# The samples' state scaled before its first use, and the decays' rows of all heads transposed once and broadcast from memory

## The chip, the cores and the metric

One kernel on one core of a Trainium2 chip. The metric is the device time of one execution in microseconds (us), lower is better. TensorE is called PE here, its weight loads PEld, VectorE DVE, ScalarE ACT, GpSimd POOL and SyncE, which issues most of the DMAs, SP.

## What is computed

One inference step of a hybrid decoder layer, for a prompt of 512 tokens and 8 samples of one token each. The width is 2048. One input projection feeds two mixers of 8 heads by 128: dilated window attention (A), and gated DeltaNet (B). The outputs go through a gate, one output projection and a norm. Everything is float32. The parts of mixer B that matter here are these two:

```python
# prompt: decay matrix of a chunk, from the cumulated logarithms of the per-head decays
gcum = jnp.cumsum(gc, axis=-1)
decay = jnp.exp(jnp.where(incl, gcum[..., :, None] - gcum[..., None, :], -jnp.inf))
a_mat = jnp.where(strict, einsum('bhnid,bhnjd->bhnij', kbeta, kc) * decay, 0.0)
...
# samples: one step on the state S (k x v) that each sample brings along
v_new = u_i - einsum('bhcd,bhde->bhce', w_i, state)
o_i = einsum('bhcd,bhde->bhce', q_i, state) + einsum('bhcj,bhje->bhce', qk_i, v_new)
state = state * gt_i[..., None, None] + einsum('bhcd,bhce->bhde', k_i, v_new)
```

`w_i` and `q_i` carry the token's decay `exp(g)`, so for one token all three terms with the state are terms with the decayed state: `v_new = beta (v - k S')`, the new state is `S' + k v_new`, and the output is `q` times the new state, where `S' = exp(g) S`.

## The kernel before

**Order of the work.** Two axes are walked: head by head (h = 0 to 7), and in each head 8 tiles of the input projection (j = 0 to 7). A tile is computed in 8 segments, 4 groups of the contraction for the first 256 tokens and 4 for the other 264. Every engine runs its own program through the same 64 turns of a head: in each turn `step(work)` advances a list of generators, each of which issues what stands up to its next `yield`. `yield from idle(n)` lets n turns pass. So the order on each engine is written out by hand, and engines meet by semaphores only. Heads 1 to 7 are a hardware loop on all engines but PE. In the text, "turn n" is the n-th of the 64 calls of a head, from 0; turn n of PE follows its segment n. A generator that begins with `idle(24)` issues its first work in turn 24.

**The projection.** Each weight tile is loaded (`w_raw`), ACT makes its high part (`w_hi`, function `hi`, L1029), and DVE and POOL take turns to make the low part (`w_lo`, function `lo`, L1396 and L2006). PE multiplies high and low parts with both parts of the tokens (L651 to L659). SP reloads `w_raw` once a low part is done (`wait_lo`). DVE takes the first half of a tile out of PSUM (L1427), ACT the second (L1059).

**The decay matrix.** `gates` (first head only) makes the cumulated logarithms of the decays of all heads, `G6[:, 1]` (128 tokens x 4 chunks x 8 heads). POOL copies those of the head into `hg`. In turn 23 PE transposes the keys (L802) and then the four columns `hg[:, 1, c]`, each spread over 128 columns (L806), which gives rows in PSUM, the same in every partition, in `mx(3)`. In turn 24 DVE subtracts the column from them (L1626) into `b_D` and masks (L1627); ACT takes the exponential (L1236). In turn 25 DVE makes `b_kb` from the keys (L1635), and PE transposes that in turn 26 (L816). `b_D` is last read in its head by DVE at L1726, turn 37, which signals `mix_QK`.

**The solve.** From turn 34 on, six levels n = 1 to 6 of a triangular inverse take three turns each: PE's product L844 (turn 34, 37, 40, 43, ...), ACT's copy, PE's L853, ACT's copy, DVE's update L1676 (turn 35, 38, 41, ...), PE's transposes L859 and DVE's update L1680 (turn 36, 39, 42, ...). The next L844 waits for both updates (`mix_UT`). POOL makes the masked operand of a level (L2055).

**The samples' state.** `delta_decode` on four engines. SP loads the keys' rows of the head, spread over the partitions (`k_rows`, L520, turn 19), the state `S0` (L526, turn 24), the queries' rows (`q_rows`, L534, turn 38), and stores the state (L538, turn 47). DVE reduces state times keys in turns 35 and 36 (L1740 in `fused`, eight blocks), makes small vectors of width 8 in turn 37 (L1777 to L1783), adds the update to the state in turns 41 to 43 (L1787, blocks 0 to 2, 3 and 4, 5 to 7), and reduces state times queries in turns 44 to 46. ACT scales the state by the decay in turns 37 and 38 (L1285, four blocks each) between the two. `fused` writes its products to `q_rows`, which are not used.

**SP's queue** around turns 16 to 24 of a head: four small stores of the keys, the probabilities' rows out (L444), a conv row out (L481), a weight load, the output of mixer A of the head before (`scratch_g<-gA`, L512, turn 18), the probabilities' rows in, three times 512 KB (L449, turns 19 to 21), and `k_rows`.

Of the kernel before, what the change touches and what calls it, by code (L numbers as in the profile page):

```python
# [157 lines left out]
def idle(n):  # L158
    for _ in range(n):
        yield  # L160
# [13 lines left out]
def build(nc, x_prompt, x_sample, cache_k, cache_v, state_conv, state_delta, g_pre, w_in, w_ba, conv_w, a_log, dt_bias,  # L174
# [5 lines left out]
    scratch_dq = nc.dram_tensor("scratch_dq", (NH, NB, HD), F32, kind="Internal").ap()  # L180
    scratch_g = nc.dram_tensor("scratch_g", (KT, P, TP), F32, kind="Internal").ap()

    with ExitStack() as ctx:
# [52 lines left out]

        small = sb("small", [P, 4 * P])
# [4 lines left out]
        gw = small[:, 0:160].rearrange("p (a c h) -> p a c h", a=4, c=NC + 1)  # L242
        gt = small[:, 160:240].rearrange("p (c a h) -> p c a h", a=2, c=NC + 1)
# [9 lines left out]
        k_rows = gx[:].rearrange("p a t -> p (a t)")  # L253
        q_rows = sb("q_rows", [P, WA])
# [73 lines left out]
        def mx(n):  # L328
# [17 lines left out]
            "hg_ok mix_T1 mix_ss mix_lnrk mix_rs mix_scal mix_gb mix_tok mix_kbT_ps mix_kbT mix_arg mix_D "  # L346
# [27 lines left out]
        def _(sp):  # L374
# [138 lines left out]

            def delta_decode(h):
                yield from idle(16)
                sp.wait_ge(s["q_row"], 3 * h + 1)
                rows_to(scratch_dk[h])
                yield from idle(3)
                sp.wait_ge(s["qrow_out"], 192 * h + 64)
                sp.dma_start(k_rows, scratch_dk[h].rearrange("b d -> (b d)").partition_broadcast(P)).then_inc(  # L520
                    s["dk_in"], 16)
                yield from idle(5)
                if not isinstance(h, int) or h > 0:
                    sp.wait_ge(s["S0_out"], 16 * h)
# [12 lines left out]
                sp.wait_ge(s["d_add"], h + 1)  # L537
                sp.dma_start(st_s[0, :, h].rearrange("b e d -> e b d"), S0[:]).then_inc(s["S0_out"], 16)  # L538
# [17 lines left out]
            stretch(0, [conv_out(0), attn_out(0), attn_rows(0), delta_decode(0)])  # L556
            with repeat(sp, 1, NH - 1) as h:
                stretch(h, [rows_out(h - 1), attn_decode(h - 1), conv_out(h), attn_out(h), attn_rows(h), delta_decode(h)])
            h = NH - 1
            stretch(h, [rows_out(h - 1), attn_decode(h - 1), conv_out(h), attn_out(h), attn_rows(h), delta_decode(h),  # L560
# [62 lines left out]
        def _(pe):  # L623
# [104 lines left out]
            def gates():  # L728

                yield from idle(8)  # L730
                pe.wait_ge(s["proj_sb"], 3)
                pe.wait_ge(s["consts"], 80)
                pe.wait_ge(s["memset_ok"], 2)
                for c in range(NC):
                    pe.matmul(MX[:, 0, c * 16:(c + 1) * 16], xba[:, c * P:(c + 1) * P], two_parts[:], start=True,
                              stop=True)
                pe.matmul(MX[0:NB, 0, 64:80], xba[:, TP:TT], two_parts[:], start=True, stop=True).then_inc(
                    s["gates_pe"], 1)
                yield from idle(5)
                pe.wait_ge(s["gates_dve"], 2)  # L740
                g = gw[:, 3, 0:NC, :].rearrange("p c h -> p (c h)")
                pe.matmul(MX[:, 1, 0:32], upper[:], g, start=True, stop=True)
                pe.matmul(MX[:, 1, 32:64], ones[:], g, start=True, stop=True).then_inc(s["gates_pe"], 1)
                yield from idle(3)
                pe.wait_ge(s["gates_dve"], 5)
                pe.matmul(MX[:, 0, 0:P], ones[0:NB, :], dgs.rearrange("p a h b -> p (a h b)"), start=True,
                          stop=True).then_inc(s["gates_pe"], 1)
# [43 lines left out]
            def mix_b(h):  # L791
# [12 lines left out]
                pe.wait_ge(s["hg_ok"], h + 1)  # L804
                for c in chunks:
                    last = pe.transpose(mx(3)[:, c, :], hg[:, 1, c:c + 1].to_broadcast((P, P)), ident[:])  # L806
                last.then_inc(s["mix_gb"], 1)
# [106 lines left out]
            def delta_decode(h):  # L914
# [6 lines left out]
                yield from idle(14)  # L921
# [96 lines left out]
        def _(act):  # L1018
# [116 lines left out]
            def gates():  # L1135
# [24 lines left out]
                act.wait_ge(s["gates_pe"], 3)  # L1160
                act.activation(bgs[:].rearrange("p a h b -> p (a h b)"), MX[:, 0, 0:P], ACT.Copy).then_inc(
# [116 lines left out]
            def delta_decode(h):  # L1278
                yield from idle(36)
                act.wait_ge(s["d_sum"], h + 1)  # L1280
                rsqrt(dd[:, 9:11, :], MD[:, 1, 0:2 * NB].rearrange("p (a b) -> p a b", a=2), 1.0, s["d_rs"])
                yield
                act.wait_ge(s["d_ks"], h + 1)
                for b in range(NB):
                    last = act.activation(S0[:, b, :], S0[:, b, :], ACT.Copy, scale=dd[:, 11, b:b + 1])  # L1285
                    if b == 3:
                        yield
                last.then_inc(s["S0_scaled"], 1)
                yield from idle(11)
                act.wait_ge(s["d_sq"], h + 1)  # L1290
                rsqrt(dd[:, 10, :], MD[:, 1, 16:24], 1.0 / HD, s["d_rs2"])
# [98 lines left out]
        def _(dve):  # L1390
# [230 lines left out]
            def mix_b(h):  # L1621
# [3 lines left out]
                dve.wait_ge(s["mix_gb"], h + 1)  # L1625
                link(dve.tensor_tensor(b_D, mx(3), bc(hg[:, 1, :]), ALU.subtract))  # L1626
# [123 lines left out]
            def delta_decode(h):  # L1750
# [4 lines left out]
                if not first:  # L1755
                    dve.wait_ge(s["qrow_out"], 192 * h)
                dve.transpose(qrow[:], xk[:, TT - 32:TT]).then_inc(s["q_row"], 1)
                yield from idle(18)
                dve.wait_ge(s["q_silu"], h + 1)
                if first:  # L1760
                    dve.wait_ge(s["gates_act"], 5)
# [4 lines left out]
                dve.tensor_copy(bt_s(0), bgs[:, 0, h, :])  # L1766
                dve.tensor_copy(bt_s(1), bgs[:, 1, h, :])
# [3 lines left out]
                dve.wait_ge(s["S0_in"], 16 * h + 16)  # L1771
# [6 lines left out]
                link(dve.tensor_tensor(dd[:, 6, :], dd[:, 6, :], bt_s(1), ALU.mult))  # L1778
# [5 lines left out]
                yield from idle(4)  # L1784
                dve.wait_ge(s["S0_scaled"], h + 1)
                for b in range(NB):
                    last = dve.scalar_tensor_tensor(S0[:, b, :], k_rows[:, b * P:(b + 1) * P], dd[:, 4, b:b + 1],  # L1787
                                                    S0[:, b, :], ALU.mult, ALU.add)
                    if b in (2, 4):
                        yield  # L1790
                last.then_inc(s["d_add"], 1)
                yield
                dve.wait_ge(s["d_add"], h + 1)
                dve.wait_ge(s["dq_in"], 16 * h + 16)
                yield from fused(None, q_rows, q_rows, dd[:, 1], (3, 6))
# [3 lines left out]
                yield from idle(3)  # L1799
# [77 lines left out]
            with repeat(dve, 1, NH) as h:  # L1877
                ch.at(h, 1, 49)
# [248 lines left out]
```

## Time and profile before

| | |
|---|---|
| Median of 3 runs | 1182.35 us (1182.23 to 1183.67) |
| The profiled execution | 1183.6 us |
| its span, first to last instruction | 1181.8 us |
| PE busy | 1146.7 us, 97% |
| DVE busy | 828.2 us, 70% |
| ACT busy | 492.8 us, 42% |
| POOL busy | 276.2 us, 23% |
| TensorE clock granted | 0.995 of full speed |
| DMA | 172.63 MB, 146 GB/s over the span |

The profile is one execution. "Busy" is the union of an engine's instructions; products on PE overlap, so starts of instructions tell more than their durations. A wait is put down to the event that came last before the waiting instruction. "DMA to landing" is the time from the issue on the queue to the semaphore that tells of the arrival.

### The profile page before, as it was taken

How to read it: one execution, taken by the hardware profiler on the slowest of the kernel's cores; microseconds unless marked ns; L12 is line 12 of the kernel's file. 1: busy time of each engine (PE TensorE's matmuls, PEld its weight loads, DVE VectorE, ACT ScalarE, POOL GpSimd, SP SyncE). 2: the span in 40 equal slices, each digit the busy share in tenths (PEclk: the TensorE clock that was granted, in tenths of full speed). 3: DMA queues.
4: the chain of work that ended last, by engine and by line, in shares of the span. 5: the costliest groups of instructions: out<-in, count | busy, mean ns of one | idle time of the engine just before them, and what ended most of it. 6: DMA issues, size and time to landing. Idle time of an engine off the chain costs nothing.

```text
span 1181.8 us, 24834 instructions
## 1 busy us (share of the span) xinstructions
PE 1146.7 (97%) x8241; PEld 1066.8 (90%) x8241; DVE 828.2 (70%) x2226; ACT 492.8 (42%) x1272; POOL 276.2 (23%) x251
## 2 busy tenths in 40 slices
PE   4999999999999999999999999999999999999997
PEld 4899989998999899989998999899998989999996
DVE  4587578777776777677777776778676877665544
ACT  5544345533543454344434443444344445322211
POOL 0223112311231123113211221222122212221211
PEclk9999999999999999999999999999999999999999
DMA  7243446344635363536253625453545374523263
GB/s 254 88 117 99 146 137 197 101 152 130 206 91 171 111 216 91 181 98 217 84 181 120 204 86 186 124 184 104 178 119 180 109 270 139 161 72 107 72 215 145
DMA packets 86635, 172.63 MB, mean 146 GB/s; under 512 B 14034, under 2 KB 24115, under 8 KB 84979
## 3 DMA queue, kind: packets, MB, share of 16 engines
q1 hardware_dynamic: 85246, 169.92, 45.5%
q10 hardware_dynamic: 1312, 1.59, 0.4%
q8 instruction: 60, 0.98, 0.4%
q14 instruction: 17, 0.13, 0.0%
HBM read 153.17 MB, written 17.44 MB: 144 GB/s over the span
## 4 chain that ended last, share of the span: by engine, by line
PE 88%; DVE 5%; issue 3%; ACT 2%; DMA 1%; SPq 0%; DVEq 0%; ACTq 0%
PE PJ L655 20%; PE PJ L651 11%; PE PJ L652 11%; PE PJ L653 11%; PE PJ L656 10%; PE MX L844 2%; PE PJ L956 2%; PE PJ L957 2%; PE MX L765 2%; PE PJ L958 2%; PE MX L853 2%; PE MX L785 1%; PE PJ L659 1%; DVE kvq L1824 1%; DVE S L1787 1%
## 5 line engine op out<-in xcount | busy, mean ns | idle before, releaser
L655 PE MATMUL PJ<-h,w_hi 128*128 128x512 f32 x1110 | 418.6, 413 | 1.4 <-DVE memx L1427 1.4
L2006 POOL TENSOR_TENSOR w_lo<-w_raw,w_hi 128x512 fp32r<-128x512 f32 x160 | 216.3, 1352 | 795.9 <-ACT w_hi L1029 795.1
L651 PE MATMUL PJ<-h,w_hi 128*128 128x264 f32 (+1 forms) x1216 | 359.7, 296 | 0.0
L652 PE MATMUL PJ<-h,w_hi 128*128 128x264 f32 (+1 forms) x1216 | 345.8, 284 | 0.0
L653 PE MATMUL PJ<-h,w_lo 128*128 128x264 f32 (+1 forms) x1216 | 345.4, 284 | 0.0
L656 PE MATMUL PJ<-h,w_lo 128*128 128x256 f32 x1110 | 311.0, 280 | 0.0
L655 PEld LDWEIGHTS PJ<-h,w_hi 128*128 128x128 f32 x1110 | 209.0, 188 | 44.2 <-DVE w_lo L1396 1.7
L1029 ACT ACTIVATE w_hi<-w_raw 128x512 fp32r<-128x512 f32 x320 | 196.8, 623 | 86.7 <-PE PJ L653 73.5
L652 PEld LDWEIGHTS PJ<-h,w_hi 128*128 128x128 f32 x1216 | 230.5, 190 | 1.5
L651 PEld LDWEIGHTS PJ<-h,w_hi 128*128 128x128 f32 x1216 | 230.2, 189 | 0.3
L653 PEld LDWEIGHTS PJ<-h,w_lo 128*128 128x128 f32 x1216 | 229.2, 188 | 0.0
L656 PEld LDWEIGHTS PJ<-h,w_lo 128*128 128x128 f32 x1110 | 209.4, 189 | 2.8 <-issue 1.7
L1396 DVE TENSOR_TENSOR w_lo<-w_raw,w_hi 128x512 fp32r<-128x512 f32 x160 | 117.0, 737 | 37.6 <-ACT w_hi L1029 34.9
L1598 DVE SCALAR_TENSOR_TENSOR memx<-memx,cw 128x512 f32<-128x512 f32 x72 | 74.9, 1041 | 2.0
L1045 ACT ACTIVATE memx<-memx 128x520 f32<-128x520 f32 x32 | 20.4, 637 | 117.1 <-DVE memx L1604 117.1
L1427 DVE TENSOR_REDUCE memx<-PJ 128x256 f32<-128x512 f32 x63 | 43.2, 686 | 28.8 <-DMA out<-memx 28.5
L1244 ACT ACTIVATE mem<-MX 128x256 f32<-128x256 f32 x48 | 18.4, 384 | 106.5 <-PE MX L844 106.5
L1824 DVE CUSTOM_DVE_ANT_0 kvq<-kvq 128x128 f32<-128x128 f32 x192 | 59.5, 365 | 0.3 <-DMA kvq<-in_cache_win_k 0.3
L2055 POOL TENSOR_TENSOR mem<-mem,levels 128x256 f32<-128x256 f32 x48 | 44.0, 922 | 31.4 <-PE MX L844 16.1
L956 PE MATMUL PJ<-h,w_hi 128*128 128x256 f32 (+1 forms) x160 | 47.6, 298 | 2.2 <-DVE h L1885 2.1
L1676 DVE TENSOR_TENSOR mem<-mem 128x256 f32<-128x256 f32 x40 | 23.4, 585 | 34.6 <-ACT mem L1248 34.1
L957 PE MATMUL PJ<-h,w_hi 128*128 128x256 f32 (+1 forms) x160 | 45.8, 286 | 0.0
(320 smaller groups left out, 1680.4 us busy)
## 6 DMA issues: line engine op xcount, KB each, us to landing
w_raw<-in_w_in SPq DMA_DIRECT2D x256, 256.0 KB, 2.8
w_raw<-in_w_out SPq DMA_DIRECT2D x64, 256.0 KB, 2.9
kvq<-in_cache_win_k SPq DMA_DIRECT2D x24, 512.0 KB, 4.7
kvq<-in_cache_win_v SPq DMA_DIRECT2D x24, 512.0 KB, 4.0
mem<-scratch_p SPq DMA_DIRECT2D x24, 512.0 KB, 7.0
out<-memx SPq DMA_DIRECT2D x16, 260.0 KB, 4.8
mem<-in_x_prompt SPq DMA_DIRECT2D x4, 1024.0 KB, 10.1
gx<-scratch_dk SPq DMA_DIRECT2D x8, 512.0 KB, 6.3
```

Of the source, the lines that this page charges most:

```text
L651: pe.matmul(ps, wh, h_hi[:, k, tok], start=k == 0, stop=False)
L652: pe.matmul(ps, wh, h_lo[:, k, tok], start=False, stop=False)
L653: last = pe.matmul(ps, wl, h_hi[:, k, tok], start=False, stop=end)
L655: pe.matmul(both, wh, h2[:, :, k, tok], start=k == 0, stop=False)
L656: last = pe.matmul(ps, wl, h_hi[:, k, tok], start=False, stop=False)
L956: pe.matmul(out, wh, h_hi[:, k, tok], start=start and i == 0, stop=False)
L957: pe.matmul(out, wh, h_lo[:, k, tok], start=False, stop=False)
L1029: act.activation(w_hi[:, par, 4 * q:4 * q + 4, :], w_raw[:, q, :, :], ACT.Copy).then_inc(s["w_hi_ok"], 1)
L1396: dve.tensor_tensor(w_lo[:, par, 4 * q:4 * q + 4, :], w_raw[:, q, :, :], w_hi[:, par, 4 * q:4 * q + 4, :].bitcast(F32), ALU.subtract).then ...
L1598: link(dve.scalar_tensor_tensor(acc[:, 0:TP], xq[:, i:i + TP], w[:, 24 + i:25 + i], acc[:, 0:TP], ALU.mult, ALU.add))
L1824: last = dve.tensor_tensor_reduce(out=x, in0=x, in1=qb[:, b * HD:(b + 1) * HD], scale=1.0, scalar=0.0, op0=ALU.mult, op1=ALU.add, accum_ou ...
L2006: pool.tensor_tensor(w_lo[:, par, 4 * q:4 * q + 4, :], w_raw[:, q, :, :], w_hi[:, par, 4 * q:4 * q + 4, :].bitcast(F32), ALU.subtract).the ...
```

## The change

Two changes are made at once.

1. **Decays' rows.** `gates` transposes `G6[:, 1]` once, to 32 rows (chunk by head) of 128; ACT copies them to `g_rows`, the first 32 partitions of `q_rows`; in turn 17 of head 0 SP stores them to memory (`scratch_c`, four small DMAs), and in turn 18 of every head loads the four rows of the head, spread over 128 partitions, into `b_D` (256 KB). DVE's L1626 takes its first input from `b_D` and waits for that DMA. The four transposes L806 and PE's wait for `hg` go.
2. **State.** ACT scales `S0` in turns 33 and 34, before the reduction with the keys, which now gives the decayed product, so DVE's small product with the decay (L1778) goes. L1787 moves to turns 38 (blocks 0 to 2) and 39 (the other five), the reduction with the queries to turns 41 to 44, its end to turn 45; PE's sum of squares moves from turn 49 to 47, ACT's root from 49 to 48. DVE's two copies of the samples' beta and decay move from turn 33 to 15. The rest of the changed kernel is as before, but for where `k_rows` and `q_rows` are declared.

```diff
+            def decay_rows(h):
+                yield from idle(17)
+                if isinstance(h, int) and h == 0:
+                    sp.wait_ge(s["gates_act"], 5)
+                    for c in range(NC):
+                        sp.dma_start(scratch_c[:, c, :], g_rows[c * NH:(c + 1) * NH, :]).then_inc(s["g_row_out"], 16)
+                else:
+                    sp.wait_ge(s["mix_QK"], h)
+                yield
+                sp.wait_ge(s["g_row_out"], 16 * NC)
+                sp.dma_start(b_D.rearrange("p c d -> p (c d)"),
+                             scratch_c[h].rearrange("c i -> (c i)").partition_broadcast(P)).then_inc(s["mix_gb"], 16)
...
+                pe.transpose(MX[0:NC * NH, 1, P:2 * P], G6[:, 1].rearrange("p c h -> p (c h)"), ident[:])
...
-                pe.wait_ge(s["hg_ok"], h + 1)
-                for c in chunks:
-                    last = pe.transpose(mx(3)[:, c, :], hg[:, 1, c:c + 1].to_broadcast((P, P)), ident[:])
-                last.then_inc(s["mix_gb"], 1)
...
-                yield from idle(14)
+                yield from idle(12)
                 pe.wait_ge(s["d_vec"], h + 1)
...
+                act.activation(g_rows, MX[0:NC * NH, 1, P:2 * P], ACT.Copy)
...
             def delta_decode(h):
-                yield from idle(36)
-                act.wait_ge(s["d_sum"], h + 1)
-                rsqrt(dd[:, 9:11, :], MD[:, 1, 0:2 * NB].rearrange("p (a b) -> p a b", a=2), 1.0, s["d_rs"])
-                yield
-                act.wait_ge(s["d_ks"], h + 1)
+                yield from idle(33)
+                act.wait_ge(s["q_row"], 3 * h + 1)
+                act.wait_ge(s["S0_in"], 16 * h + 16)
                 for b in range(NB):
                     last = act.activation(S0[:, b, :], S0[:, b, :], ACT.Copy, scale=dd[:, 11, b:b + 1])
                     if b == 3:
                         yield
                 last.then_inc(s["S0_scaled"], 1)
-                yield from idle(11)
+                yield
+                yield
+                act.wait_ge(s["d_sum"], h + 1)
+                rsqrt(dd[:, 9:11, :], MD[:, 1, 0:2 * NB].rearrange("p (a b) -> p a b", a=2), 1.0, s["d_rs"])
+                yield from idle(12)
...
-                dve.wait_ge(s["mix_gb"], h + 1)
-                link(dve.tensor_tensor(b_D, mx(3), bc(hg[:, 1, :]), ALU.subtract))
+                dve.wait_ge(s["mix_gb"], 16 * h + 16)
+                link(dve.tensor_tensor(b_D, b_D, bc(hg[:, 1, :]), ALU.subtract))
...
-                dve.wait_ge(s["S0_in"], 16 * h + 16)
+                dve.wait_ge(s["S0_scaled"], h + 1)
                 yield from fused(s["d_ks"], k_rows, q_rows, dd[:, 0], (5,))
...
-                link(dve.tensor_tensor(dd[:, 6, :], dd[:, 6, :], bt_s(1), ALU.mult))
...
-                yield from idle(4)
-                dve.wait_ge(s["S0_scaled"], h + 1)
+                yield
                 for b in range(NB):
                     last = dve.scalar_tensor_tensor(S0[:, b, :], k_rows[:, b * P:(b + 1) * P], dd[:, 4, b:b + 1],
                                                     S0[:, b, :], ALU.mult, ALU.add)
-                    if b in (2, 4):
+                    if b == 2:
                         yield
                 last.then_inc(s["d_add"], 1)
                 yield
+                yield
                 dve.wait_ge(s["d_add"], h + 1)
                 dve.wait_ge(s["dq_in"], 16 * h + 16)
-                yield from fused(None, q_rows, q_rows, dd[:, 1], (3, 6))
+                yield from fused(None, q_rows, q_rows, dd[:, 1], (2, 3, 6))
...
-                yield from idle(3)
+                yield from idle(5)
                 dve.wait_ge(s["z_ok_b"], h + 1)
```

## Rows read from the trace of the kernel before

**Rows 1.** the page, busy us (share of the span) xinstructions
```profile
PE 1146.7 (97%) x8241; PEld 1066.8 (90%) x8241; DVE 828.2 (70%) x2226; ACT 492.8 (42%) x1272; POOL 276.2 (23%) x251
```

**Rows 2.** waits of PE and PEld: who for whom, us in total, times, longest
```profile
PE MX L844 <- DVE mem L1680: 4.6, 8, 1.2
...
PEld MX L844 <- issue: 8.7, 16, 1.5
```

**Rows 3.** line L806: engine, count, ns min/median/max, first and last start
```profile
L806 PE MATMUL MX<-ident,hg x32: 272/273/273, 78.7 to 893.2; 128*128 128x128 f32 x32
```

**Rows 4.** timeline of PE: start us, us, engine line op out<-in
```profile
427.51 0.60 PE L802 MATMUL MX<-ident,memx 128*128 128x128 f32 x4
...
428.30 0.47 PE L655 MATMUL PJ<-h,w_hi 128*128 128x512 f32 x1
...
429.77 0.60 PE L811 MATMUL MX<-ident,memx 128*128 128x128 f32 x4
430.13 0.48 PE L655 MATMUL PJ<-h,w_hi 128*128 128x512 f32 x1
...
433.01 0.60 PE L816 MATMUL MX<-ident,mem 128*128 128x128 f32 x4
...
452.32 0.61 PE L844 MATMUL MX<-mem 128*128 128x128 f32 x4
...
458.65 0.61 PE L844 MATMUL MX<-mem 128*128 128x128 f32 x4
...
464.62 0.68 PE L844 MATMUL MX<-mem 128*128 128x128 f32 x4 [0.48 <-DVE mem L1680]
```

**Rows 5.** timeline of DVE, 429 to 432 us
```profile
429.17 0.68 DVE L1626 TENSOR_TENSOR mem<-MX,hg 128x512 f32<-128x512 f32 x1
...
431.42 0.69 DVE L1635 TENSOR_TENSOR mem<-MX,sk 128x512 f32<-128x512 f32 x1
```

**Rows 6.** timeline of the DMA issues on SP
```profile
426.45 0.33 SPq L512 DMA_DIRECT2D scratch_g<-gA  x1
427.03 0.35 SPq L449 DMA_DIRECT2D mem<-scratch_p  x1
...
460.63 0.33 SPq L534 DMA_DIRECT2D q_rows<-scratch_dq  x1
```

**Rows 7.** DMA issues of the span: count, KB each, median us to landing
```profile
w_raw<-in_w_in SPq DMA_DIRECT2D x256, 256.0 KB, 2.8
...
q_rows<-scratch_dq SPq DMA_DIRECT2D x8, 512.0 KB, 4.1
...
scratch_g<-gA SPq DMA_DIRECT2D x7, 256.0 KB, 3.2
```

**Rows 8.** line L449, the DMA mem<-scratch_p of 512 KB
```profile
DMA to landing us min/median/max: 4.5/7.0/8.8
```

**Rows 9.** timeline of ACT, 446 to 458 us
```profile
446.86 0.38 ACT L1244 ACTIVATE mem<-MX 128x256 f32<-128x256 f32 x1 [3.40 <-PE MX L844]
447.13 0.62 ACT L1029 ACTIVATE w_hi<-w_raw 128x512 fp32r<-128x512 f32 x1
...
456.69 1.28 ACT L1285 ACTIVATE S<-S,dd 128x128 f32<-128x128 f32 x4
```

**Rows 10.** timeline of DVE, 449 to 464 us
```profile
449.13 0.89 DVE L1676 TENSOR_TENSOR mem<-mem 128x256 f32<-128x256 f32 x1 [2.35 <-ACT mem L1248]
...
451.06 0.42 DVE L1680 TENSOR_TENSOR mem<-mem,MX 128x256 f32<-128x256 f32 x1
...
457.44 0.42 DVE L1680 TENSOR_TENSOR mem<-mem,MX 128x256 f32<-128x256 f32 x1 [0.57 <-PE MX L859]
...
462.24 1.90 DVE L1787 SCALAR_TENSOR_TENSOR S<-gx,dd,S 128x128 f32<-128x128 f32 x3
```

**Rows 11.** timeline of POOL; in brackets its idle time before and what ended it
```profile
458.57 1.28 POOL L2006 TENSOR_TENSOR w_lo<-w_raw,w_hi 128x512 fp32r<-128x512 f32 x1 [8.83 <-ACT w_hi L1029]
```

**Rows 12.** line L1787 in the head from 411 to 527 us, ns
```profile
L1787 DVE SCALAR_TENSOR_TENSOR S<-gx,dd,S x8: 341/348/1371, 462.2 to 467.4; 128x128 f32<-128x128 f32 x8
```

More of the change, by code:

```diff
@@ L180, in build @@
     scratch_dq = nc.dram_tensor("scratch_dq", (NH, NB, HD), F32, kind="Internal").ap()
+    scratch_c = nc.dram_tensor("scratch_c", (NH, NC, P), F32, kind="Internal").ap()
     scratch_g = nc.dram_tensor("scratch_g", (KT, P, TP), F32, kind="Internal").ap()
@@ L235, in build @@
         st_prod = gx[:].rearrange("p a t -> p (a t)")[:, 0:9 * NH * NB].rearrange("p (m b i) -> p m b i", m=3 * NH, i=3)
+        k_rows = gx[:].rearrange("p a t -> p (a t)")
+        q_rows = sb("q_rows", [P, WA])
         small = sb("small", [P, 4 * P])
@@ L242, in build @@
         gw = small[:, 0:160].rearrange("p (a c h) -> p a c h", a=4, c=NC + 1)
+        g_rows = q_rows[0:NC * NH, 0:P]
         gt = small[:, 160:240].rearrange("p (c a h) -> p c a h", a=2, c=NC + 1)
@@ L252, in build @@
         rb = sb("rb", [NB, 5 * P])
-        k_rows = gx[:].rearrange("p a t -> p (a t)")
-        q_rows = sb("q_rows", [P, WA])
         pd = rb[0:NB, P:4 * P].rearrange("p (n t) -> p n t", n=3)
@@ L344, in build @@
             "cw_ok crow_out conv_ok conv_sig kv_silu q_silu "
-            "hg_ok mix_T1 mix_ss mix_lnrk mix_rs mix_scal mix_gb mix_tok mix_kbT_ps mix_kbT mix_arg mix_D "
+            "hg_ok g_row_out mix_T1 mix_ss mix_lnrk mix_rs mix_scal mix_gb mix_tok mix_kbT_ps mix_kbT mix_arg mix_D "
             "mix_kk mix_qk mix_A mix_QK mix_B mix_U0 mix_T_ps mix_T mix_Y_ps mix_Y mix_Z mix_Zs mix_UT ch_kS ch_r "
@@ L554, in early_rows @@
                     load_row(k)
-            stretch(0, [conv_out(0), attn_out(0), attn_rows(0), delta_decode(0)])
+            stretch(0, [conv_out(0), attn_out(0), attn_rows(0), delta_decode(0), decay_rows(0)])
             with repeat(sp, 1, NH - 1) as h:
-                stretch(h, [rows_out(h - 1), attn_decode(h - 1), conv_out(h), attn_out(h), attn_rows(h), delta_decode(h)])
+                stretch(h, [rows_out(h - 1), attn_decode(h - 1), conv_out(h), attn_out(h), attn_rows(h), delta_decode(h), decay_rows(h)])
             h = NH - 1
-            stretch(h, [rows_out(h - 1), attn_decode(h - 1), conv_out(h), attn_out(h), attn_rows(h), delta_decode(h),
+            stretch(h, [rows_out(h - 1), attn_decode(h - 1), conv_out(h), attn_out(h), attn_rows(h), delta_decode(h), decay_rows(h),
                         early_rows()], last=True)
@@ L1754, in delta_decode @@
                 dve.wait_ge(s["kv_silu"], 2 * h + 1)
-                if not first:
+                if first:
+                    dve.wait_ge(s["gates_act"], 5)
+                else:
                     dve.wait_ge(s["qrow_out"], 192 * h)
+                dve.tensor_copy(bt_s(0), bgs[:, 0, h, :])
+                dve.tensor_copy(bt_s(1), bgs[:, 1, h, :])
                 dve.transpose(qrow[:], xk[:, TT - 32:TT]).then_inc(s["q_row"], 1)
@@ L1759, in delta_decode @@
                 dve.wait_ge(s["q_silu"], h + 1)
-                if first:
-                    dve.wait_ge(s["gates_act"], 5)
                 dve.tensor_tensor(dd[:, 2, :], kd, kd, ALU.mult)
@@ L1765, in delta_decode @@
                 dve.transpose(qrow[:], cq[:, TT - 32:TT]).then_inc(s["q_row"], 1)
-                dve.tensor_copy(bt_s(0), bgs[:, 0, h, :])
-                dve.tensor_copy(bt_s(1), bgs[:, 1, h, :])
                 yield
@@ L1877, in _ @@
             with repeat(dve, 1, NH) as h:
-                ch.at(h, 1, 49)
+                ch.at(h, 1, 48)
                 stretch(h, [tail_a(h - 1), mix_b(h), own_b(h), own_a(h), mix_q(h), delta_decode(h),
```

## The prediction, made before the changed kernel was run

> **What bounds the kernel now.** I began with the page's busy times [rows 1]: TensorE (PE) works in 97% of the span, so the question is what PE no longer has to do, and where it will wait. The waits of PE and of its weight loads come next [rows 2]: in the steady heads there is one real stall, at the solve's product L844, once per head, behind the vector engine's (DVE's) update L1680. It adds up to 4.6 us on PE in 8 heads. The weight loads show 8.7 us of idle time in 16 places at the same line: this stall and a second, small one per head. The instructions of L806 [rows 3] give the period: from the first head to the last, (893.2 - 78.7) / 7 = 116.4 us. The heads repeat nearly to the tenth, so I read one of them, that from about 411 to 527 us, and multiply. In it I went through the timelines of PE, DVE, the DMA issues, ScalarE (ACT) and GpSimd (POOL) around the places that the change touches. "Turn n" below is a call of every engine's step function; a head has 64 of them.
>
> **The four transposes leave PE.** With them, PE needs from 427.51 (L802) to 428.30 (the next projection) 0.79 us; an equal group of four alone (L811) needs 429.77 to 430.13, 0.36 us [rows 4]. So 0.43 us leave each head, 3.4 us in 8. This is on the bounding engine, and it is worth this only if nothing on the way gets later. The one transpose added in `gates` and ACT's copy of its result come once, and cost some 0.2 us at most.
>
> **What takes their place is a DMA.** b_D is now filled by a 256 KB broadcast that SP issues in turn 18, behind a weight load and the output of gA, issued at 426.45 [rows 6]. So it goes out at about 427.0, where the broadcast of the probabilities goes now, and that and `k_rows` behind it go 0.55 us later. These two are read 20 turns on or more, so this costs nothing. The wait on mix_QK in turn 17 is for the head before and is long met; behind it in SP's queue stand only those same issues. The landing is not shown by the trace. From below: 256 KB weight loads take 2.8 us at the median [rows 7], which gives 429.8. From above: the 512 KB broadcast issued at this very place takes at least 4.5 us [rows 8], that is 431.5; half the bytes may be under a microsecond less. The gA write ahead of it needs 3.2 us [rows 7] and is down at 429.65, and the row can hardly be earlier. I take 430.6, between that and the broadcast, nearer to the first as the size is the same. DVE now reads the argument at 429.17 (L1626) [rows 5]. It will start at about 430.7, 1.55 us late.
>
> Behind that wait in DVE's order stand L1627, a low weight part, and then L1635, which makes b_kb. It ran from 431.42 to 432.11 with no gap in which the delay could vanish; it will end at 433.66. PE transposes b_kb (L816) from 433.01 on [rows 4], its first weight load 0.12 us before; without L806 it would be there 0.43 us sooner. PE will load at about 433.7 instead of 432.89: **net +0.8 us a head**, the saved transposes counted. At the bounds the net is +0.0 (429.8) and +1.7 (431.5).
>
> The Trainium skill ("DMA: Bandwidth & Descriptors", Latency and other measured facts) puts the fixed cost of a DMA at about 2 us, the less the lighter the load. By that and 0.65 us for the bytes the row would land at 429.7 and this term would be about -0.1 instead of +0.8, the whole sum some 6 us less. The trace's gA row, 3.2 us for the same bytes, speaks for later.
>
> **The state's scaling goes ahead.** ACT now scales the eight blocks in turns 37 and 38; 4 of them take 1.28 us [rows 9]. They move to turns 33 and 34. Turn 33 costs nothing, as ACT idles 3.40 us there, until 446.86. Those of turn 34 stand before the high weight part at 447.13 [rows 9], which ends 1.2 us later, and POOL's low part behind it will run from about 449.0 to 450.3. DVE's solve update L1676 (449.13, 0.89 us [rows 10]) reads SBUF twice. Operations of this kind do not run beside POOL's here: of the eight L1787 in this head seven take about 0.35 us and the one that met a POOL operation 1.37 [rows 12]; in the group of three that it heads (1.90 us) the other two follow in 0.27 us each [rows 10]. So L1676 ends near 450.5, the five reductions behind it (now 1.1 us, from the end of L1676 to L1680 at 451.06) hold POOL's next operation off once and end near 452.0, and L1680, 0.4 us long, about 452.4. PE asks for it 0.12 us before its product at 452.32 [rows 4]: **+0.25**, between 0 and 0.5.
>
> The Trainium skill says the same of the two engines ("SBUF — State Buffer", Who interferes with whom): a DVE instruction with two SBUF inputs contends with POOL for a shared port, held as a lock for the whole instruction. It would spare L1680, one of whose inputs is in PSUM. It also speaks against this change in that L1626 loses its PSUM input, but POOL is idle when it runs.
>
> **The state's update goes ahead too.** One small DVE product falls away (0.2 us, in idle time), two copies move earlier (0.15 us, idle too). The eight L1787 move from turns 41 to 43 to turns 38 and 39. Three of them now stand before L1680 of turn 39, which ran at 457.44 after 0.57 us of idle time [rows 10] and may start by about 458.1, for PE's product at 458.65 [rows 4]. DVE is free for them from 456.87; alone they need 0.27 us each. But ACT's high weight part of this turn, freed of the scaling, ends 1.2 us earlier [rows 9], and POOL's low part, which waits for it and starts at 458.57 now [rows 11], starts at 457.3. It falls between the second and the third L1787 and holds the third until 458.6; L1680 then ends at 459.15, PE wanted it at 458.55: **+0.55**, between 0 and 0.8.
>
> What is gained is the old stall. L1680 of turn 42 runs behind three L1787 that end at 464.14 [rows 10], and PE stands until 464.62 [rows 4], 4.6 / 8 = 0.6 us a head [rows 2], so it could have gone on at 464.0. Now two reductions over the queries' rows stand there, and these rows are wanted in turn 41, not 44. They are issued at 460.63 [rows 6] and take 4.1 us [rows 7], so 464.7, against DVE's arrival at 462.3. The issue waits for POOL's low part of turn 38, which is 1.2 us earlier, so 463.5; with two reductions of 0.21 us (1.1 / 5) and L1680 behind, PE goes on about 0.4 us late instead of 0.6, **-0.25** with the shift of PE's own time. The second stall, at most (8.7 - 4.6) / 8 = 0.5 us a head [rows 2], I take for 0.2, as most of what a weight load idles is covered by the product before it; it goes, as DVE has less in turns 42 to 44: **-0.2**.
>
> **Sum.** A steady head: 0.8 + 0.25 + 0.55 - 0.25 - 0.2 = +1.15, times 7 is +8.0. In head 0 the rows must first go to memory and back (four small DMAs, then the broadcast); the landing is about 1.7 us behind DVE's need, and the net with the rest is +0.9. Together +9: span 1181.8 to about 1190.8 by the profiled execution; it took 1183.6 us in all, the median of the runs shown is 1182.35. I add the 9 to the median: **1191.3 us**.
>
> **Rivals.** The first ends on the other side: the broadcast lands by about 429.5 and POOL's part misses the L1787. Then PE keeps the 3.4 us of the transposes (less 0.1 a head for what DVE is late), the old stalls of 0.6 + 0.2 us a head go, 6.4 us, and the time is 1182.35 - 9 = 1173.5, or up to 1179 with part of it. For it: the stall really is behind L1787, and a 256 KB load alone takes 2.8 us. Against: gA ahead in the queue. It decides at a landing of about 429.7, if no more than one collision with POOL happens.
>
> The second is that both cancel: landing near 429.9 (0 to +0.1 a head), one collision with POOL (+0.5), the old stalls gone (-0.6): 1181 to 1184.
>
> The third: POOL's part of turn 38 is not earlier, and so SP's issue of the queries' rows is not. They land at 464.7; DVE, in order, holds L1680 behind them until 465.3, and PE stands 1.5 us there instead of 0.6. That is +0.9 + 0.25 = +1.15 more a head, 1200.5. Against it: the scaling that held ACT in turn 38 is plainly gone.
>
> That the transposes leave and their time is not seen would be the second rival; nothing in the diff suggests that they stay.
>
> **Chances.** Forecast, 1186 to 1197: 0.50. First rival, 1173 to 1180: 0.25. Second: 0.14. Third and worse, 1198 to 1205: 0.11. A measurement of this kernel can tell about 0.2% (2.4 us) from no change. So faster 0.25, same 0.14, slower 0.61. The range for 8 in 10 is 1176 to 1200: it takes in most of the faster case, since the landing bound alone moves the sum by 7 us either way.
>
> **What would show it.** Right: DVE idles about 1.5 us before L1626's successor, released by the DMA into mem; the weight load of the b_kb transposes waits for DVE about 1.2 us in each head; L844 of turn 40 waits about half a microsecond, with an L1787 of over 1 us next to a POOL row; the period from head to head becomes 117.4 to 117.6 us. Wrong: no idle time of DVE there (landing by 429.2), or PE gaps gone and a period of 115.2. If the largest wait is on the queries' rows in turn 41, the third rival holds.

## The result, and the profile after

The changed kernel takes **1201.14 us** (median of 4 runs, 1197.03 to 1205.38), the kernel before 1182.64 in the same session (1182.23 to 1183.67): a ratio of 1.0156, 95% interval 1.0135 to 1.0177. It is slower by 18.5 us. I had forecast slower by 9, and a range up to 1200; the sign was right, the size was not, and the time lies just outside the range. Its profiled execution took 1201.52 us, with a span of 1199.7, 17.9 more than before. All times below are medians of all executions, but the ratios leave out four slow ones of 1257 to 6435 us (one each of e2, e3, e8 and the kernel before).

In the changed kernel L844 is L857, L816 is L829, L1626 is L1642, L1635 is L1651, L1676 and L1680 are L1692 and L1696, L1787 is L1801, and the reductions are L1756. The page's busy times and then the waits of PE, of its weight loads and of DVE, as in [rows 1, 2]:

```profile
PE 1149.6 (96%) x8210; PEld 1064.7 (89%) x8210; DVE 829.1 (69%) x2218; ACT 491.5 (41%) x1273; POOL 275.5 (23%) x251
```

```profile
DVE mem L1642 <- DMA mem<-scratch_c: 18.8, 8, 3.7
...
PEld MX L829 <- DVE mem L1651: 16.7, 8, 3.3
...
PE MX L829 <- DVE mem L1651: 14.1, 8, 2.9
...
PE MX L857 <- DVE mem L1696: 5.9, 8, 1.9
```

Two lines did not exist before: DVE waits in every head for the decays' rows, 18.8 us in all, and PE hands that on before it transposes b_kb, 14.1 us. The old stall, 4.6 us in 8 heads [rows 2], has not gone; it is 5.9. The line of the load itself, its issues and its landings:

```profile
L527 SPq DMA_DIRECT2D mem<-scratch_c x8: 354/355/430, 78.0 to 908.9; - x8
...
DMA to landing us min/median/max: 3.3/4.4/5.9
```

One head, the third, on the timeline (start, duration, engine; in brackets the idle time before and what ended it):

```profile
315.98 0.38 SPq L381 DMA_DIRECT2D w_raw<-in_w_in  x1
...
316.55 0.33 SPq L514 DMA_DIRECT2D scratch_g<-gA  x1
...
317.07 0.35 SPq L527 DMA_DIRECT2D mem<-scratch_c  x1
...
317.68 0.35 SPq L451 DMA_DIRECT2D mem<-scratch_p  x1
...
318.22 0.33 SPq L536 DMA_DIRECT2D gx<-scratch_dk  x1
...
322.56 0.69 DVE L1642 TENSOR_TENSOR mem<-mem,hg 128x512 f32<-128x512 f32 x1 [3.26 <-DMA mem<-scratch_c]
...
324.76 0.69 DVE L1651 TENSOR_TENSOR mem<-MX,sk 128x512 f32<-128x512 f32 x1
...
325.51 0.66 PE L829 MATMUL MX<-ident,mem 128*128 128x128 f32 x4 [2.69 <-DVE mem L1651]
```

The load goes out 1.09 us behind a weight load and 0.52 behind gA's output, as the prediction said, but DVE starts at 322.56, 5.5 us after the issue, and PE stands 2.7 us. Windows of that stretch (PE, PEld, DVE, ACT, POOL busy, granted clock, DMA share, GB/s):

```profile
320.00:327.00 7.00, 4.31 (x26) 3.49 (x25) 4.37 (x9) 2.66 (x8) 0.00 (x0) 0.99 0.95 296
327.00:331.00 4.00, 4.00 (x22) 3.90 (x21) 3.20 (x4) 0.95 (x2) 1.57 (x1) 0.59 1.00 374
331.00:335.00 4.00, 4.00 (x36) 4.00 (x35) 2.78 (x6) 1.80 (x3) 0.66 (x1) 1.00 0.13 50
```

Two things beside the stall are seen here. The 16 DMA engines are 95% busy around the landing, so the row shares them with other transfers. And right after the stall the granted clock of TensorE averages 0.59 over 4 us; between 327 and 330 it is 0.50, which is 1.2 GHz instead of 2.4. PE makes 22 products in these 4 us instead of 36, which costs (1 - 0.59) x 4 = 1.6 us more.

### The profile page after: what moved, and what is told of

It reads as the page before. It is cut to its first block and busy times, and to the rows that moved or that the text cites. A ratio compares the mean times of both kernels' runs of the same rounds, so it can differ in the third digit from the quotient of the medians.

```text
span 1199.7 us, 24783 instructions
## 1 busy us (share of the span) xinstructions
PE 1149.6 (96%) x8210; PEld 1064.7 (89%) x8210; DVE 829.1 (69%) x2218; ACT 491.5 (41%) x1273; POOL 275.5 (23%) x251
## 5 line engine op out<-in xcount | busy, mean ns | idle before, releaser
L1412 DVE TENSOR_TENSOR w_lo<-w_raw,w_hi 128x512 fp32r<-128x512 f32 x160 | 114.0, 718 | 37.8 <-ACT w_hi L1042 35.2
L1258 ACT ACTIVATE mem<-MX 128x256 f32<-128x256 f32 x48 | 18.5, 385 | 109.2 <-PE MX L857 109.2
L1692 DVE TENSOR_TENSOR mem<-mem 128x256 f32<-128x256 f32 x40 | 24.4, 609 | 48.3 <-ACT mem L1262 48.3
L2070 POOL TENSOR_TENSOR mem<-mem,levels 128x256 f32<-128x256 f32 x48 | 42.3, 888 | 28.3 <-PE MX L857 16.6
```

Of the source, the lines that this page charges most:

```text
L1412: dve.tensor_tensor(w_lo[:, par, 4 * q:4 * q + 4, :], w_raw[:, q, :, :], w_hi[:, par, 4 * q:4 * q + 4, :].bitcast(F32), ALU.subtract).then ...
```

## The experiments

The theory from these rows: most of the loss is the row's landing, 4.6 us on average and not 3.6; the rest is the queries' rows, which come late in some heads, and the scaling in turn 34. Rivals: the state's new order costs the most; gA's output ahead of the row makes it late; the read of one small row by 128 partitions makes it slow; what is issued behind it does. The kernel before took 1183.07, 1183.46 and 1182.92 us in the three sessions.

| run | time, us | ratio to before (95%) |
|---|---|---|
| e1 rows' part alone | 1199.09 (1195.36 to 1199.71) | 1.0116 (1.0090 to 1.0143) |
| e2 state's part alone | 1186.25 | 1.0020 (1.0007 to 1.0033) |
| e3 row loaded in turn 7 | 1188.64 | 1.0040 (1.0024 to 1.0057) |
| e4 gA's output later | 1194.89 | 1.0090 (1.0070 to 1.0110) |
| e5 another source | 1196.32 | 1.0108 (1.0088 to 1.0127) |
| e6 e3, scaling in turn 33 | 1184.29 | 1.0010 (0.9996 to 1.0024) |
| e7 e6, queries' rows in turn 37 | 1177.03 (1175.59 to 1177.71) | 0.9940 (0.9927 to 0.9953) |
| e8 e7 with the transposes | 1181.98 | 0.9983 (0.9970 to 0.9995) |
| e9 transfers behind it later | 1195.42 | 1.0112 (1.0075 to 1.0148) |
| e10 those and gA later | 1188.65 | 1.0057 (1.0040 to 1.0074) |
| e11 queries' rows in turn 37 alone | 1197.58 (1191.90 to 1204.07) | 1.0108 (1.0075 to 1.0141) |

### Each half alone (e1, e2)

e1 is the kernel before with point 1 of the change, e2 with point 2.

> The kernel before with only the first half of the change: the decays' rows by broadcast in turn 18, the state's order as before. Theory 'late row': nearly the whole loss is here, since TensorE's transposes of b_kb wait for the vector engine, which waits for the row; the changed kernel shows 15.4 us more at that place, 3.4 us less for the transposes, 1.6 us less for a wait of the kernel before in its last head. So 1193 to 1199 us, and a wait of about 2 us a head before the transposes of b_kb. Rival 'state order': the row costs what was forecast, 6 us, and the rest comes with the state: 1186 to 1190 us.

> The kernel before with only the second half: state scaled first, updates in turns 38 and 39, the four transposes kept. Theory 'late row': 0.28 us a head more at the solve's second product, behind ScalarE's scaling in turn 34, which is 2.2 us, and up to 1.5 us in one or two heads where the queries' rows land late, less the old stalls: 1181 to 1186 us. Rival 'state order': 1190 us or more.

e1 is 1.16% slower, e2 0.20%; together 1.36%, and the whole change is 1.56%. So the rows' part carries most of it. Both times lie a little above the ranges of theory 'late row' (by 0.1 and 0.25 us) and far from those of the rival. In e1 PE waits as in the full change, its second line being the old stall, unchanged at 4.5 us:

```profile
PE MX L829 <- DVE mem L1649: 12.6, 8, 2.9
...
PE MX L857 <- DVE mem L1694: 4.5, 8, 1.2
```

### The row loaded early (e3)

```diff
             def decay_rows(h):
-                yield from idle(17)
+                yield from idle(17 if isinstance(h, int) and h == 0 else 6)
```

> The changed kernel with one number changed: in heads 1 to 7 the broadcast of the decays' rows is issued in turn 7 instead of 18; head 0 as it was. The same DMA, the same bytes, no transposes. Theory 'late row': the waits before the transposes of b_kb vanish in heads 1 to 7, 13.3 us, and the 1.5 us that the halved clock cost after one of them: 1184 to 1188 us. Rival 'added traffic': the DMA and what it displaces cost wherever it stands: 1192 us or more. If the landing takes 2.8 to 3.2 us here, the 4.6 us of turn 18 are the queue's; if it stays above 4, the broadcast itself is slow.

1188.64, 12.5 us less than the changed kernel. Only head 0, whose load stayed in its place, still waits before L829:

```profile
PE MX L857 <- DVE mem L1696: 5.4, 8, 1.7
...
PE MX L829 <- DVE mem L1651: 3.1, 1, 3.1
```

That places about two thirds of the 18.5 us on the landing (by the ratios, 1.16 of 1.56 points). Only the moment of the load was altered, and the two profiles have the two parts: 11.0 us less of PE's waits before L829, and no stretch at a lower clock behind them. The time is 0.6 us above the range of 'late row', and far below the 1192 of 'added traffic'. But the expectation had also set a test for the landing, and it came out on the other side: in turn 7 the load takes 3.3/4.7/5.7 us (min/median/max), not 2.8 to 3.2. By that test the broadcast itself would be slow, or turn 7 is no quiet place either; e5 decides.

### What makes the landing late (e4, e5, e9, e10)

e4 moves gA's output from turn 18 to 24 (`idle(14)` to `idle(20)`).

> The changed kernel with the output of gA (256 KB written) issued in turn 24 instead of 18, so that it no longer stands ahead of the row's broadcast. Theory 'queue ahead': the row lands about 1 us sooner, in 3.6 us, and the time falls by 6 to 9 us to 1192 to 1195 us. Theory 'small source': the landing takes its time because 128 partitions read the same 2 KB beside the other broadcasts; it stays at 4.2 us or more and the time at 1197 us or more.

The row goes out one slot earlier, but from issue to landing it still needs 3.9 to 5.1 us, 4.6 at the median. PE's waits at L829 fall to 9.9 us and the time by 6.2 us. So 1194.89 lies in the range of 'queue ahead', but its mechanism did not come: the gain is the earlier issue, and gA ahead of the row is by itself not what makes it slow. Nor did the 1197 us of 'small source' come; the next run tests that theory.

e5 reads another source, so its kernel does not load the decays' rows:

```diff
-                             scratch_c[h].rearrange("c i -> (c i)").partition_broadcast(P)).then_inc(s["mix_gb"], 16)
+                             w_in[0, 0].rearrange("p a b -> p (a b)")).then_inc(s["mix_gb"], 16)
```

> The changed kernel, with one thing altered: the load into b_D reads 256 KB of w_in, every partition its own 2 KB, in place of the same 2 KB row of scratch_c for all 128 partitions. Size, place in the queue and waits are the same; the decays' values, and so the output, are not the reference's. Theory A (the many reads of one small row make the broadcast slow): from issue to landing it takes 2.8 to 3.3 us, as a plain load of its size, instead of 4.6; the wait before the b_kb transposes falls by 1.3 to 1.6 us a head, and the kernel takes 1188 to 1191 us. Theory B (what the other transfers of this stretch do to it, whatever it reads): 4.2 to 4.8 us to the landing, and 1199 to 1202 us.

The landing of this plain load (e5), the line of its issue:

```profile
DMA to landing us min/median/max: 3.4/4.6/5.2
```

No faster than the broadcast's 3.3/4.4/5.9. The means are 4.4 and 4.6 us, with heads from 3.3 to 5.9. Theory A falls: the small source read 128 times costs nothing that can be seen, and the place decides. The time, 1196.3, was below theory B's 1199 to 1202: DVE's waits for the load were 16.8 us instead of 18.8.

e9 puts what is issued right behind the row four turns later. (The expectation speaks of 768 KB; `k_rows` too is 512 KB, so it is 1 MB.)

```diff
-            def attn_decode(hh, at=12, out=5, back=2):
+            def attn_decode(hh, at=12, out=5, back=6):
...
                 rows_to(scratch_dk[h])
-                yield from idle(3)
+                yield from idle(7)
```

> The changed kernel with what is issued right behind the broadcast put four turns later: the 512 KB tiles of the probabilities and the keys' rows; the output of gA and the weight load ahead of it stay. Theory A (the broadcast shares the DMA engines with the 768 KB issued within 1.2 us behind it): it lands 3.2 to 3.9 us after its issue in place of 4.6, the wait before the b_kb transposes falls by about 1 us a head, and the kernel takes 1191 to 1195 us. Theory B (what counts is what is in flight ahead of it): 4.4 to 4.8 us, 1198 to 1202 us.

e10 moves gA's output as well (to turn 30; the expectation says 26).

> The same with the output of gA put off too (turn 26), so that only the weight load stands beside the broadcast. Theory A as before (behind it): 3.0 to 3.6 us to the landing and an issue one slot earlier, the wait before the transposes under 0.5 us a head, 1186 to 1190 us. Theory B (ahead of it): only now does the landing fall, and by itself as much as this. Theory C (neither; a row read by 128 partitions into this tile needs its 4.5 us): 4.4 us or more, with the issue earlier some 1194 us.

The landings of e9 and then of e10:

```profile
DMA to landing us min/median/max: 3.3/4.1/4.6
```

```profile
DMA to landing us min/median/max: 3.0/3.4/4.6
```

Over heads 1 to 7, which have these neighbours, the means are 4.6 us in the changed kernel, 4.5 in e4, 4.0 in e9 and 3.3 in e10. In e9 the landing fell by 0.6, less than theory A wanted, and its time is just above A's. In e10 it is what A gave, and the time falls another 6.8 us, to 1188.65 (a part of it since the row also goes out one slot earlier). So neither neighbour alone explains it: with both gone the 256 KB need 3.3 us, with the 1 MB behind it alone 4.5, with gA ahead alone 4.0, and with both 4.6 (a weight load is ahead in all four). These are means of seven heads of one profile each. The same neighbours as in the changed kernel gave 4.4, 4.4 and 4.7 in e1, e5 and e11, so 4.5 and 4.6 are no difference, while 4.0 and 3.3 lie below all of them. That the transfers share the engines, 95% busy in the windows above, fits this, but how they share them no row shows. PE's waits of e10:

```profile
PE MX L857 <- DVE mem L1696: 6.0, 8, 1.6
...
PE MX L829 <- DVE mem L1651: 2.3, 2, 2.1
```

Early loading in e7 shows that what is ahead can be enough: two weight loads and gB's output stand within 1.8 us ahead of the row there, nothing for 2.7 us behind it, and in heads 1 to 7 it lands in 4.5 to 5.2 us; in head 0, with nothing ahead in flight, in 3.3. There nobody waits for it.

### The queries' rows and the scaling (e11, e6)

e11 takes the wait for the key reduction off the load of the queries' rows: the reduction's unused products go to gB and gA, once these have been sent out. In the order of the turns that is one turn earlier (37 instead of 38), but on the queue more: in the fourth head the load was issued 0.94 us behind the solve's product of turn 40, and is now issued 2.41 us behind that of turn 37, 4.9 us earlier. (The expectation of e7 says four turns; there it is 5.6 us, some three.)

```diff
-                sp.wait_ge(s["d_ks"], h + 1)
-                yield
                 sp.wait_ge(s["qrow_out"], 192 * h + 128)
                 sp.dma_start(q_rows[:], scratch_dq[h].rearrange("b d -> (b d)").partition_broadcast(P)).then_inc(
...
-                    last = dve.tensor_tensor_reduce(out=out[:, b * P:(b + 1) * P], in0=S0[:, b, :],
+                    o = out[:, b * P:(b + 1) * P] if x is None else (gB, gA)[b // 4][:, b % 4 * P:(b % 4 + 1) * P]
+                    last = dve.tensor_tensor_reduce(out=o, in0=S0[:, b, :],
```

> The changed kernel with the queries' rows asked for in turn 37, and nothing else altered (the key reduction writes its unused products over gB and gA). Theory A (the rows are late where TensorE waits most at L857): those waits fall from 5.9 us to under 4, the landing in time in every head, and the kernel takes 1196 to 1199 us. Theory B (the waits at L857 are those of the scaling in turn 34 alone): 1200 to 1202 us, the waits as before.

1197.58, in theory A's range, with an interval that still reaches to the changed kernel; the waits say it more clearly. First the timeline of the changed kernel in its fourth head:

```profile
474.10 0.41 DVE L1692 TENSOR_TENSOR mem<-mem 128x256 f32<-128x256 f32 x1
...
477.16 0.29 DVE L1756 CUSTOM_DVE_ANT_0 q_rows<-S,q_rows 128x128 f32<-128x128 f32 x1 [2.65 <-DMA q_rows<-scratch_dq]
...
477.59 0.42 DVE L1696 TENSOR_TENSOR mem<-mem,MX 128x256 f32<-128x256 f32 x1
...
478.15 0.68 PE L857 MATMUL MX<-mem 128*128 128x128 f32 x4 [1.90 <-DVE mem L1696]
```

and here the waits of e11 (L855 is L857, L827 is L829):

```profile
PE MX L827 <- DVE mem L1649: 15.5, 8, 3.6
PE MX L855 <- DVE mem L1694: 2.9, 8, 1.1
```

The solve's waits fall from 5.9 to 2.9 us, the longest, 1.1, being that of head 0. DVE stood 2.65 us for the queries' rows with L1696 behind that wait; in e11 nobody waits for them.

e6 is e3 with all eight scalings in turn 33, and head 0's load three turns earlier.

```diff
                     last = act.activation(S0[:, b, :], S0[:, b, :], ACT.Copy, scale=dd[:, 11, b:b + 1])
-                    if b == 3:
-                        yield
                 last.then_inc(s["S0_scaled"], 1)
-                yield
-                yield
+                yield from idle(3)
```

> The changed kernel with the broadcast ten turns earlier (turn 7; head 0 in turn 14) and all eight scalings of the state in turn 33. Theory A (the four scalings in turn 34 put off the high weight part, POOL's low part and DVE's solve update behind them): the second L857 is on time again and the time is 2 us below the 1188.6 that the early broadcast alone gave, 1185.5 to 1187.5. Theory B (the 0.28 us there comes from elsewhere, such as DVE's own order): 1188 to 1190.

It took 1184.29 us, below both theories, 4.3 less than e3. The expectation left out that head 0's wait of 3.1 us goes too; with it A would have given some 5.3 less. That it was only 4.3 fits the solve's waits, which are longer in its profile:

```profile
PE MX L857 <- DVE mem L1693: 9.1, 8, 2.1
```

They are those for the queries' rows. Their load is issued 0.94 us behind the product of turn 40 in e3 as in e6, but it takes longer to land, first in e3, then in e6 (the line of its issue, L550):

```profile
DMA to landing us min/median/max: 3.5/3.8/5.1
```

```profile
DMA to landing us min/median/max: 3.5/4.5/5.5
```

Four of the eight land in 4.9 us or more in e6, one in e3. Whether the new order does that or chance does, one profile of each can't tell. e6 altered two things at once, so it doesn't settle the scaling's price by itself.

### All together, and without the rows' part (e7, e8)

e7 is e6 with e11's edit; e8 is point 2 of the change with both edits and the four transposes kept.

> As the run with the early broadcast and the early scaling, and the queries' rows are asked for in turn 37, four turns before they are now: the key reduction no longer writes its unused products over them but over gB and gA, so that nothing holds the transfer. Theory A (the rest of the loss against the kernel before is the late queries' rows): the waits at L857 go but for traces (under 1 us in all), and with the transposes gone the kernel takes 1174 to 1179 us, faster than before by 0.4% to 0.7%. Theory B (the update's and the reductions' new places in DVE's order cost by themselves): L857 waits 3 us or more, and 1181 to 1185 us.

> The state's part of the change alone, the four transposes kept, with the scaling in turn 33 and the queries' rows in turn 37. Theory A: it lies above the run that also has the early broadcast by what the four transposes take on TensorE, 0.43 us in 8 heads, 3.4 us: 1177 to 1182 us. Theory B (b_D's reads and the transfer cost the other kernel as much as the transposes): both take the same within 1 us.

e7 takes **1177.03 us, 0.6% faster than the kernel before** (interval 0.47% to 0.73%); its waits:

```profile
PE MX L855 <- DVE mem L1691: 2.9, 8, 1.1
...
PE PJ L967 <- DVE h L1899: 2.1, 1, 2.1
```

L829's wait is gone and the solve's is at 2.9. Theory A of e7 holds in time; it wanted under 1 us of waits, and overlooked head 0's 1.1 us and a quarter of a microsecond in the others. e8 is 5.0 us above e7, against 3.4 for the transposes: in theory A's range by its time, above the 3.4 by its difference. In the two profiles, 5.6 us apart, PE's starts side by side give 0.43 us in each head for the transposes; 0.9 us in the last head, where e8 has the wait shown below and e7 has none; and some 1.1 us near the end, where e8's granted clock is 0.66 from 968 to 973 us and e7's stays at 1.00.

```profile
PE PJ L653 <- DVE memx L1424: 0.7, 1, 0.7
```

So the rows' part, placed well, is a gain of what the transposes took and about 1 us more; the clock's part is of these two executions and no gain of the change.

## Why the prediction was right and wrong

The sum by place, forecast for seven heads and the landing for eight. "Measured" is by PE's start-to-start distances in the two profiled traces laid side by side; it adds up to the 17.9 us between the spans.

| step | forecast, us | measured, us |
|---|---|---|
| landing, transposes counted | +6.5 | +15.4 - 3.4 = +12.0 |
| scaling in turn 34, second product | +1.8 | +2.2 |
| three L1787 and POOL, turn 40 | +3.9 | 0 |
| old stalls, turn 43 | -3.2 | +1.5 |
| clock after the stalls | none | +1.6 |
| all else, a wait of 1.6 us gone in the last head | 0 | +0.6 |

**The landing: right in mechanism, wrong in size, and the step that failed.** The issue was 0.52 us behind gA, DVE's order behind the wait was as told, and PE's transposes waited in each head. The eight added gaps are 2.12, 3.11, 2.85, 1.60, 1.25, 0.68, 2.50 and 1.30 us. I had taken 3.6 us from issue to landing, "between that and the broadcast, nearer to the first as the size is the same". It was 4.6 on average, beyond my upper bound of 4.5 in four heads of eight (4.56, 5.87, 5.46 and 5.12 us). One microsecond in 8 heads is 8 us by itself, more than the 5.5 by which this term was missed; the chain behind the landing was 0.3 us a head shorter than I had it. The signs named say the same: DVE idled 2.35 us a head for the row and not 1.5, the weight load of the transposes waited 2.1 and not 1.2, and the period was 118.7 us and not 117.4 to 117.6. The median of 256 weight loads, 2.8 us [rows 7], was taken over the whole span, and I never asked for those of this stretch. [Rows 8] held the warning, 7.0 us at the median, and I used its minimum as the upper bound. What I should have read is this, in the kernel before: the weight load's line between 425.5 and 426.4 us, and then between 428 and 433:

```profile
DMA to landing us min/median/max: 3.2/3.2/3.2
```

```profile
DMA to landing us min/median/max: 5.9/7.8/8.2
```

The same 256 KB that land in 3.2 us when issued at 425.87 need 5.9 and more from 428.8 on. A row issued at 427.0 lies between them, by a straight line at 3.2 + 2.7 x 1.15 / 2.9 = 4.3 us, which would have been my value, an estimate, with a bound of 5.9 above it. The Trainium skill ("DMA: Bandwidth & Descriptors", Latency and other measured facts) has some 2 us fixed. With my 0.65 for the bytes that estimate, 2.65, is near the weight loads of the kernel before, 2.5 us at the least and 2.8 at the median, but not near this load: the least of eight was 3.3 us, and no run gave less than 3.0.

**The four transposes: right,** 0.43 us a head.

**The scaling in turn 34: right.** The chain came as worked out, here in the fourth head:

```profile
458.90 1.27 ACT L1297 ACTIVATE S<-S,dd 128x128 f32<-128x128 f32 x4
460.07 0.62 ACT L1042 ACTIVATE w_hi<-w_raw 128x512 fp32r<-128x512 f32 x1
460.76 1.29 POOL L2021 TENSOR_TENSOR w_lo<-w_raw,w_hi 128x512 fp32r<-128x512 f32 x1 [3.79 <-ACT w_hi L1042]
...
460.99 1.36 DVE L1692 TENSOR_TENSOR mem<-mem 128x256 f32<-128x256 f32 x1 [2.70 <-ACT mem L1262]
```

L1692 takes 1.36 us beside POOL instead of 0.89 [rows 10], and the second product came 0.28 us later in each head. One reading behind this was wrong: of the eight L1787 [rows 12] six took about 0.35 us and not seven. Another, at 465.38, took 0.83, and it too had a POOL operation beside it, so the reading's error speaks for the mechanism.

**L1787 against POOL in turn 40: wrong, by a hair.** I forecast +0.55 a head; PE shows no wait there. The three updates and the low part in the same head:

```profile
468.90 0.87 DVE L1801 SCALAR_TENSOR_TENSOR S<-gx,dd,S 128x128 f32<-128x128 f32 x3
...
469.51 1.41 POOL L2021 TENSOR_TENSOR w_lo<-w_raw,w_hi 128x512 fp32r<-128x512 f32 x1 [6.64 <-ACT w_hi L1042]
469.69 0.41 DVE L1696 TENSOR_TENSOR mem<-mem,MX 128x256 f32<-128x256 f32 x1
470.02 2.95 DVE L1801 SCALAR_TENSOR_TENSOR S<-gx,dd,S 128x128 f32<-128x128 f32 x5
```

The third update was under way when POOL began, in every head, by about 0.1 us, and each of the three took 0.35 us. The collision came all the same, with the five of the next turn, beside this low part and the two POOL operations behind it (L2070): three of the five take 1.05, 0.76 and 0.76 us in each head, where the line's median is 0.35, but PE waits for nothing behind them. A mechanism with a tenth of a microsecond of clearance deserves a chance, not a term in the sum.

**The old stalls: wrong in sign.** In five heads PE comes 0.1 to 0.2 us sooner, in head 0 nothing changes, and in heads 1 and 3 (counted from 0) the queries' rows come late: +0.95 and +1.42. The gain was sized too high to begin with: 4.6 / 8 = 0.6 us a head hides that head 0 has 1.2 and the others 0.48, and with the queries' rows in time (e7, e11) 1.1 and 0.25 us of them stay. And I had reckoned with one landing, the median of 4.1; it lies between 3.5 and 5.3 us, 4.85 in head 1 and 5.32 in head 3, so that DVE waits 0.8 to 2.65 us for these rows in every head, 10.3 in all. The third rival had named this outcome, DVE holding L1680 behind the rows, but not its cause: it wanted an issue that is not earlier, and the issue did come 1.05 us earlier (0.94 us behind the product of turn 40, 1.99 before), as forecast. Nor are these waits the largest, which its sign asked for: the row's are, 18.8 us. The landing (+5.5 beyond the forecast) and this (+4.7) outweigh the collision that cost nothing (-3.9); with 2.6 for the clock, the scaling and the rest the sum came out 9 too low in the spans. The rival's time, 1200.5, is close to the result, but by luck, with other terms.

**The clock** was in no step; the last section has it. The range failed because its upper end rested on a bound from a best case. The first rival, 1173.5, supposed a landing by 429.5, 2.5 us after the issue, which no load of the row did in any run (the least was 3.0); e7 reached nearly its time by issuing earlier.

## What to carry to other kernels

A transfer that takes the place of compute is priced at its own place in the queue: read how long the neighbours issued there take, the longest too, and add those that will share the engines. If it has slack, issue it many turns earlier; here that one line was worth 12.5 us, and clearing its neighbours as much. When an operation moves earlier, look for the loads that feed its successors, and move them first.

## What the runs showed of the hardware that was not expected

**The stall can cost twice.** Half of PE's long waits before L829 were accompanied or followed by a stretch at a lower granted clock. I took the weight load's idle time before that line in the eight profiles in which the row came late in any head (the changed kernel, e1, e3, e4, e5, e9, e10, e11). Of 64, 19 were over 2.2 us, and with 10 of those windows of 4 us with a granted clock under 0.9 came within 8 us of the wait's end; with none of the 45 shorter ones did they. Two waits alike can end either way: in the changed kernel one of 3.27 us was not followed by it, one of 3.01 was. It hit e11's profiled execution hardest, in four heads of eight (it was also the slowest of its four, 1204.07 us); here its second (PE's timeline, then windows):

```profile
208.03 0.69 PE L827 MATMUL MX<-ident,mem 128*128 128x128 f32 x2 [3.56 <-DVE mem L1649]
```

```profile
200.00:207.00 7.00, 4.47 (x28) 3.64 (x26) 2.84 (x5) 2.66 (x15) 0.00 (x0) 0.96 0.98 266
207.00:214.00 7.00, 5.97 (x27) 5.59 (x28) 5.85 (x10) 2.45 (x6) 1.28 (x1) 0.55 0.88 327
214.00:221.00 7.00, 7.00 (x57) 6.82 (x56) 4.50 (x9) 3.31 (x7) 2.10 (x2) 1.00 0.25 67
```

The 7 us from 207 on run at 0.55, which is (1 - 0.55) x 7 = 3.2 us. PE stood until 208.03, in about 0.5 of them, so some 2.7 us are lost beside the wait of 3.56. This makes these kernels uneven in part: the changed kernel's four runs span 8 us, the slowest, 1205.38, at a mean clock of 0.986. But 1201.52 and 1197.03 have the same 0.995, and e6, with no such wait, spans 7.5 us in ten runs, where the kernel before spans 1.5 us in four runs and 4.8 in the 18 of a later session. What decides between two equal waits stays open.

**A broadcast costs what a plain load costs here** (e5): the same 2 KB read for all 128 partitions took 4.6 us on average and 256 KB of distinct data 4.4, where single heads lie between 3.3 and 5.9.
